# Float32r halves for the scores of the prompt's attention in a one-core hybrid decoder step

## What is computed

```
s = jnp.einsum('nqgrd,nqkgd->nqgrk', qb.astype(jnp.float32), k_g.astype(jnp.float32)) * (HEAD_DIM ** -0.5)
s = jnp.where(valid[:, :, None, None, :], s, -jnp.inf)
p = jax.nn.softmax(s, axis=-1)
o = jnp.einsum('nqgrk,nqkgd->nqgrd', p, v_g.astype(jnp.float32))
```

## Time and profile before

| | us |
|---|---|
| median of 3 runs | 2372.76 (2372.74 to 2382.14) |
| the profiled execution | 2369.18 |
| its span, first to last instruction | 2367.5 |
| block of the prompt's attention in it | 489.6 to 664.5 |

### The profile page before, as it was taken

The page is one execution under the profiler, slowest core; times in us unless marked ns, Lnnn a source line. Parts: engine busy times, 40 slices in busy tenths (PEclk is TensorE's granted clock), DMA queues, the critical chain, the costliest instruction groups (busy, mean ns, idle before and its releaser), DMA issues. The chain is left out here.

```text
span 2367.5 us, 37205 instructions
## 1 busy us (share of the span) xinstructions
PE 2232.2 (94%) x13836; PEld 2056.8 (87%) x13836; DVE 1001.8 (42%) x2431; ACT 782.0 (33%) x1414; POOL 634.6 (27%) x387
## 2 busy tenths in 40 slices
PE   5998899589989999999999999888999999999998
PEld 4885489245578999999999999888999999999998
DVE  2525788776435433233233332357333333323323
ACT  4204577655533312212212212354122122122124
POOL 4110111257736222222222222432222222222224
PEclk8998999889999999999999999899999999999999
DMA  8454464400032111111111112001111111111112
GB/s 301 140 171 128 148 207 156 144 18 1 0 127 80 54 45 50 49 44 44 44 44 51 46 44 65 27 19 45 46 45 45 44 46 52 45 44 44 44 44 82
DMA packets 208668, 170.29 MB, mean 72 GB/s; under 512 B 14477, under 2 KB 202109, under 8 KB 208565
## 3 DMA queue, kind: packets, MB, share of 16 engines
q1 hardware_dynamic: 201917, 154.64, 21.0%
q10 hardware_dynamic: 4160, 8.65, 1.0%
q0 software_dynamic: 2496, 5.77, 0.9%
HBM read 155.85 MB, written 11.64 MB: 71 GB/s over the span
## 5 line engine op out<-in xcount | busy, mean ns | idle before, releaser
L524 PE MATMUL pair<-hhi,whi 128*128 128x352 f32 x2184 | 716.6, 328 | 33.9 <-DVE hlo L725 8.8
L525 PE MATMUL pair<-hlo,whi 128*128 128x352 f32 x2184 | 705.0, 323 | 0.0
L526 PE MATMUL pair<-hhi,wlo 128*128 128x352 f32 x2184 | 704.6, 323 | 0.0
L2143 POOL TENSOR_TENSOR wlo<-wraw,whi 128x1024 fp32r<-128x1024 f32 x127 | 304.6, 2399 | 1145.1 <-ACT whi L2088 1143.9
L524 PE MATMUL pair<-hidh,whi 128*128 128x352 f32 x1536 | 495.4, 323 | 0.0
L525 PE MATMUL pair<-hidl,whi 128*128 128x352 f32 x1536 | 492.7, 321 | 0.0
L526 PE MATMUL pair<-hidh,wlo 128*128 128x352 f32 x1536 | 492.2, 320 | 0.0
L536 DVE SCALAR_TENSOR_TENSOR x<-pair,mod,x 128x352 f32<-128x352 f32 (+1 forms) x432 | 247.4, 573 | 514.6 <-PE pair L526 513.6
L524 PEld LDWEIGHTS pair<-hhi,whi 128*128 128x128 f32 x2184 | 412.3, 189 | 45.3 <-issue 25.0
L525 PEld LDWEIGHTS pair<-hlo,whi 128*128 128x128 f32 x2184 | 413.5, 189 | 0.4
L526 PEld LDWEIGHTS pair<-hhi,wlo 128*128 128x128 f32 x2184 | 412.3, 189 | 0.5
(11 more groups left out here) (282 smaller groups left out, 1955.3 us busy)
## 6 DMA issues: line engine op xcount, KB each, us to landing
wraw<-in_w_up_dram SPq DMA_DIRECT2D x64, 512.0 KB, 3.9
wraw<-in_w_down_dram SPq DMA_DIRECT2D x64, 512.0 KB, 3.4
mraw_i<-in_w_mod_dram SPq DMA_DIRECT2D x20, 1024.0 KB, 6.8
mraw_q<-in_w_mod_dram SPq DMA_DIRECT2D x12, 1024.0 KB, 5.1
mraw<-in_w_mod_dram SPq DMA_DIRECT2D x8, 1024.0 KB, 9.2
wraw<-in_dsa_w_in_dram SPq DMA_DIRECT2D x16, 512.0 KB, 6.0
mraw_w<-in_w_mod_dram SPq DMA_DIRECT2D x8, 1024.0 KB, 5.2
wraw<-in_dsa_w_o_dram SPq DMA_DIRECT2D x16, 512.0 KB, 4.1
```

What stands on the lines that cost most here:

```text
L524: pe.matmul(out, a, hi[:, kr, r], start=(n == 0), stop=False)
L525: pe.matmul(out, a, lo[:, kr, r], start=False, stop=False)
L526: last = pe.matmul(out, b, hi[:, kr, r], start=False, stop=(n == len(ks) - 1))
L2143: pool.tensor_tensor(wlo[:, slot(k), :], wraw[:, slot(k), :], whi[:, slot(k), :], ALU.subtract).then_inc(lo_ready, 1)
```

## The change

For tiles 1 to 7 the scores of a head are now three float32r products instead of one float32 product: upper half of the queries times upper half of the keys, upper times rest, rest times upper. Tile 0 stays in float32. A product covers at least 256 keys, so that tile 4 (640 keys) computes 512 + 256 columns, as tile 5 does.

The halves are made inside the attention block, for the tile ahead, by the list `SPLITS`: 18 entries, each one ACT copy of 128 x 512 into float32r (`qh` or `kh`) and one DVE difference (`ql` or `kl`). Queries of tile t go in two entries of four heads, after heads h = 1 and h = 4 of tile t - 1; keys go in four entries of 256 columns of both groups, after head h = 2 of tiles 0, 1, 3 and 5. So tiles 0, 1, 3 and 5 hold three entries, tiles 2, 4 and 6 two, and tile 7 none. On ACT the copy stands behind the exponential of head n and ahead of the copies of head n - 3. On DVE the difference stands behind the reciprocal of head n - 1, with a wait for that ACT copy (`q_upper`). TensorE waits for the differences (`q_rest`) at the first head of each half tile.

```
--- before.py
+++ after.py
@@ -300,7 +300,10 @@
         ss = put("ss", [P, SR, SEQ])
         causal = put("causal", [P, 2 * P])
         pt = [put("pt0", [P, TILES, GROUP * P]), at("pt1", [P, TILES, GROUP * P], F32, whi.manual_sbuf_range[0])]
-        assert pt[0].manual_sbuf_range[1] <= s1 and pt[1].manual_sbuf_range[1] <= wlo.manual_sbuf_range[1]
+
+        kh, kl = (put(n, [P, KV, SEQ], F32R) for n in ("kh", "kl"))
+        qh, ql = (put(n, [P, 2, HEADS, P], F32R) for n in ("qh", "ql"))
+        assert ql.manual_sbuf_range[1] <= s1 and pt[1].manual_sbuf_range[1] <= wlo.manual_sbuf_range[1]
 
         pair = [ctx.enter_context(nc.psum_tensor(f"pair{i}", [P, 2, 512], F32)) for i in range(4)]
 
@@ -1787,6 +1790,28 @@
         qk_list = [(t, h) for t in range(TILES) for h in range(HEADS)]
         turn_list = [(t, h, a) for t, h in qk_list for a in range((t + 4) // 4)]
         PV_AFTER = AHEAD + GROUP
+
+        KW2 = 2 * P
+        SPLITS = []
+        for t in range(1, TILES):
+            n = HEADS * (t - 1)
+            SPLITS.append((n + 1, "q", t, 0))
+            if t % 2 == 0 or t == 1:
+                SPLITS.append((n + 2, "k", t // 2, None))
+            SPLITS.append((n + 4, "q", t, 1))
+        SPLIT0 = 2 * len(IDX_TILES)
+
+        def split_parts(kind, i, half):
+            if kind == "q":
+                h = slice(GROUP * half, GROUP * (half + 1))
+                return qt[:, h, i * P:(i + 1) * P], qh[:, i % 2, h, :], ql[:, i % 2, h, :]
+            c = slice(KW2 * i, KW2 * (i + 1))
+            return kt[:, :, c], kh[:, :, c], kl[:, :, c]
+
+        def splits_needed(t, h):
+
+            return max(m for m, (_, kind, i, half) in enumerate(SPLITS)
+                       if (kind == "q" and i == t and half == h // GROUP) or (kind == "k" and i <= t // 2)) + 1
         with nc.Block() as block:
             @block.sync
             def _(sp):
@@ -1804,10 +1829,20 @@
                     if n >= 2:
                         pe.wait_ge(neg_done, n - 1)
                     L = P * (t + 1)
+                    if t == 0:
+                        pe.matmul(pair[1 + n % 2][:, 0, 0:P], qt[:, h, 0:P], kt[:, h // GROUP, 0:P], start=True,
+                                  stop=True).then_inc(qk_ready, 1)
+                        return
+                    if h % GROUP == 0:
+                        pe.wait_ge(q_rest, SPLIT0 + splits_needed(t, h))
+                    a, b = qh[:, t % 2, h, :], ql[:, t % 2, h, :]
                     for s in range((L + 511) // 512):
-                        w = min(512, L - 512 * s)
-                        ins = pe.matmul(pair[1 + n % 2][:, s, 0:w], qt[:, h, t * P:(t + 1) * P],
-                                        kt[:, h // GROUP, 512 * s:512 * s + w], start=True, stop=True)
+                        w = max(KW2, min(512, L - 512 * s))
+                        r = slice(512 * s, 512 * s + w)
+                        out = pair[1 + n % 2][:, s, 0:w]
+                        pe.matmul(out, a, kh[:, h // GROUP, r], start=True, stop=False)
+                        pe.matmul(out, a, kl[:, h // GROUP, r], start=False, stop=False)
+                        ins = pe.matmul(out, b, kh[:, h // GROUP, r], start=False, stop=True)
                     ins.then_inc(qk_ready, 1)
 
                 def turn(n):
@@ -1865,6 +1900,10 @@
                         act.activation(ss[:, n % SR, 0:L], ss[:, n % SR, 0:L], ACT.Exp,
                                        bias=small[:, 4 + n % SR:5 + n % SR],
                                        scale=SC_ATT, accum_out=small[:, 8 + n % SR:9 + n % SR]).then_inc(exp_done, 1)
+                    for at_n, kind, i, half in SPLITS:
+                        if at_n == n:
+                            whole, upper, _ = split_parts(kind, i, half)
+                            act.activation(upper, whole, ACT.Copy).then_inc(q_upper, 1)
                     if n >= AHEAD:
                         copies(n - AHEAD)
 
@@ -1913,6 +1952,11 @@
                                           ALU.mult).then_inc(neg_done, 1)
                     if 1 <= n <= N:
                         recip(n - 1)
+                    for m, (at_n, kind, i, half) in enumerate(SPLITS):
+                        if at_n == n:
+                            whole, upper, lower = split_parts(kind, i, half)
+                            dve.wait_ge(q_upper, SPLIT0 + m + 1)
+                            dve.tensor_tensor(lower, whole, upper, ALU.subtract).then_inc(q_rest, 1)
                     if n >= PV_AFTER + GROUP and (n - PV_AFTER) % GROUP == 0:
                         take_pv((n - PV_AFTER) // GROUP - 1)
 
```

## The result

The change makes the kernel slower. The median goes from 2372.76 to 2396.49 us, a ratio of 1.0095 with a 95% interval of 1.008 to 1.0109. The forecast was +9 us and "no change within 0.5%", with a range that ended at 2393; +24 lies outside it. The profiled execution took 2393.02 us with a span of 2391.4.

A forecast was written before the change was run, and what follows sets the result against it. VectorE was taken to bound tiles 2 and 3, TensorE tiles 4 to 7; +14 us in tiles 0 to 3 less 2.3 and 2.6 gave +9.1, so 2382 us, no change, range 2374 to 2393.

The forecast's parts named there:

- Where the time is lost: Attention block, 18 splits: VectorE waits in order for ScalarE's copy behind the exponential; each costs 1.7 to 2.3 us.
- Tiles 0 to 3: Splits need 20.3 us of VectorE against 9.9 idle, so these tiles grow by about 14 us.
- Tiles 4 to 7: TensorE leads again; tiles 4 and 5 save nothing, tiles 6 and 7 save 2.3 and 2.6 us.
- What TensorE saves: Scores in tiles 1 to 7: float32r products save at most 9.8 us, counting only from tile 4 on.
- Nothing is won back: Rival: tiles 0 to 3 hand delays on whole, +20.3 us, 4.9 saved later, +15.4, 2388 us; chance 0.17.
- The clock: Rival: TensorE's clock falls in tiles 1 to 3, adding 2.6 us in tile 3; 2385 to 2391; chance 0.13.
- The waits are hidden: Rival: copies and differences fall into VectorE's idle time, the change gives its 9.8 us, 2363 us; chance 0.08.
- the products aren't faster: Rival: 0.1 us more per head, saving 0.8 us less in each of tiles 6 and 7; 2383.5 us; chance 0.05.
- The signs: Profile after: VectorE idle 0.9 to 1.8 us before 18 differences, tile 4 near 550, tile 7 9 to 13 us later.

The follow-up runs named there:

- the two half experiments: The change with VectorE's differences one head later in tiles 0 to 3 only, 2383.11 us, or in tiles 4 to 6 only, 2387.85 us.
- the runs of one part each: The change's splits with the float32 products of before, 2398.78 us; its three float32r products with splits only ahead of the first head, 2372.63 us.

## Why the prediction was wrong

- **Where the time is lost: right.** The loss comes from VectorE waiting in order behind ScalarE's copy. The blocking was forecast at 35.7 us in all; 23.3 of waits and 18 differences at some 0.61 make 34.3.
- **Tiles 0 to 3: right.** +14 was forecast, as 3.4, 2.9, 3.6 and 4.2; it is +15.8, as 3.6, 3.6, 3.5 and 5.0. The first reduction of tile 4 came 61.8 us after that of tile 0, against 46.0.
- **Tiles 4 to 7: the step that failed.** The prediction said that VectorE needs less than its idle time there, so that TensorE leads again and works off the lag by what it saves. It let the splits of these tiles cost only the 2.0 us that tiles 4 and 5 would have saved, and came to -4.9. It is +6.7 in tiles 4 to 6 and -1.6 in tile 7 and what follows it, +5.1. The error of 10 us is here, and its main term is the cost of these splits: alone they make tiles 4 to 6 8.1 us longer (77.8 to 85.9). The waits are most of it: without them the change's 84.5 us there become 78.3. VectorE's idle time took up about half of the burden, not nearly all of it: the seven splits hold VectorE for some 15 us (10.8 of waits in the trace of after, and seven differences at 0.61), and 8.1 come through. In part that idle time is VectorE's waiting for scores that are late because its own last maximum was late, as the chain of heads 42 and 43 shows; such time is no room. And a lag from tiles 0 to 3 is not worked off, as the two half experiments show.
- **The path that was not in the prediction.** I took the 2.7 us between GpSimd's end and the transposes for the lag that TensorE can bear. But the transposes of head n - 3 also wait for the copies of head n - 4, which stand behind the exponential of head n - 1; that wait was already among TensorE's waits in the trace of before, 4.5 us in 10 heads, and I had not put it among my rows. Most of TensorE's new waiting shows there, 16.8 us. It is not the error, though: with that path closed from tile 4 on in both kernels the change costs 20.6 us instead of 20.8.
- **What TensorE saves: half of it.** 9.8 us at the most, 6.9 of them in tiles 4 to 7, of which the forecast counted 4.9; the products alone give 4.8 and 4.3. So this term is off by less than 1 us. A product costs what the earlier trace rows say, but TensorE stood 6.7 us for the copies of the probabilities in that run, where it was 4.5, so part of the saving became waiting (its trace, the same view as above).
- **The rivals.** "Nothing is won back" was right about tiles 4 to 6 in its reason, waiting along the chain that is not free room, but placed it in tiles 0 to 3: there 4.5 of the 20.3 us were won back, in tiles 4 to 6 nothing of the 15.8 that came in. Its +15.4 for the whole is nearer to the 20.8 than the forecast, but it too let tiles 4 to 7 save 4.9. The clock did fall, to 0.71 in tile 1 and 0.92 in tile 3. The code of tiles 0 to 3 is the same in the change and in the run with later differences in tiles 4 to 6 only; there the mean clock over these tiles is 0.86 instead of 0.83, tile 3 stands at 1.00, and they take 61.8 us alike, so a price can't be seen there. It can be seen in tile 5 of that run, 1.6 us. By the Trainium skill's page "TensorE: Matmul & The Clock Gate", section "HAM oscillation — how this bites in real kernels", that fall is what happens to a TensorE kept waiting; the trace agrees on the fall, though the same wait of 2.26 us in the run with all differences late was followed by none. "The waits are hidden" fell with the result, and "the products aren't faster" with the runs of one part each.
- **The signs.** VectorE waited before all 18 differences, 0.75 to 1.66 us each, as foretold. Tile 4 started at 557.5, past the 554 that was to speak for "nothing won back"; but 5.3 us of that lie ahead of the attention, and without them it is 552.2. PEclk in tiles 2 and 3 was 1.00 and 0.92, not under 0.9. Counted in the same way tile 7 started 22.5 us late instead of 9 to 13: the sign that points at tiles 4 to 6.
- **The range** ended at +20 because every case that set it had tiles 4 to 7 save something. None held that tiles 4 to 6 add 6.7 us.

What stays open: of the 8.4 us that the volume of the splits costs without waits, 5.2 lie in tiles 0 to 3 (50.7 against 45.6) and 3.2 in tiles 4 to 6 (78.3 against 75.1); I did not part ScalarE's share from VectorE's. Nor did I close GpSimd's path together with the copies', so it isn't shown how much of the loss in tiles 4 to 6 would be left without either.

## What to carry to other kernels

When one engine's product is consumed by another in the same step of a walk, let the consumer stand one step later in its list; here that one line is worth 17 of 195 us. Idle time of an engine inside a loop of engines is room only if the loop as a whole has slack: follow a late result once round the loop, through every wait of every engine it meets, before calling it hidden. List what the leading engine waits for in the kernel before, however small: undoing the 4.5 us found there was worth 5.8 us, without any of the change. And try a cure in the kernel before as well as in the slow one: only what it gives more in the slow one belongs to the loss.

## What the runs showed of the hardware

A float32r product right behind a float32 one costs nothing extra in a stream here: in the stretch of tile 5 above, the two halves of a value product (0.86 us) and the first product of the scores together take 593.68 - 592.58 = 1.10 us, which leaves 0.24 for that product, against 0.23 behind another float32r product. The ACT copy into float32r of 128 x 512 takes 0.61 us and the difference 0.69, within 0.02 of the rows with 64 partitions in the earlier trace rows. And TensorE's idle time in the profile is too small where it waits behind a product, because records overlap. In tile 5 of the kernel before, the transposes start 1.29 us after the scores where nothing is waited for (566.16 to 567.45). In the rows below it is 1.62 us, so 0.33 are lost, and the record shows 0.17:

```profile
568.97 1.45 PE L1809 MATMUL pair<-kt,qt 128*128 128x512 f32 x4
570.59 0.85 PE L1820 MATMUL pair<-cst,ss 128*128 128x128 f32 x6 [0.17 <-ACT pt L1856]
```

So the order of ScalarE's instructions alone could take 5.8 us out of the attention, while the waits on record were 4.5.
